# A new order of the SBUF tensors in a two-layer encoder trunk: activations on multiples of 2 KB, the places of the split weights staggered by 64 bytes

## The reference, cut to what matters

```python
for l in range(DEPTH):                       # DEPTH = 2
    u = x @ w_in[l]                          # 2048 -> 6144 (even) or 6152 (odd)
    # even: GLU + causal depthwise conv (31 taps) + LayerNorm + silu | HGRN2 heads
    # odd:  forgetting attention | chunked attention with relative bias
    mix = jnp.concatenate([a_out, b_out], axis=-1) @ w_out[l]    # 2048 -> 2048
    x = layer_norm(ALPHA * x + mix, ln_mix_g[l], ln_mix_b[l])
    h = jnp.square(jax.nn.relu(x @ mlp_w1[l])) @ mlp_w2[l]       # 2048 -> 8192 -> 2048
    x = layer_norm(ALPHA * x + h, ln_mlp_g[l], ln_mlp_b[l])
```

## Time and profile before

| | |
|---|---|
| median of 3 runs | 2315.05 us (2314.43 to 2316.96) |
| span of the profiled execution, first to last instruction | 2314.1 us |
| PE busy in the span | 2251.9 us (97%) |
| granted clock of TensorE, mean | 0.988 of full speed |
| memory read | 414.79 MB, 180 GB/s over the span |

### The profile page before, as it was taken

The page is one execution under the profiler, slowest core; times in us unless marked ns, Lnnn a source line. Parts: engine busy times, 40 slices in busy tenths (PEclk is TensorE's granted clock), DMA queues, the critical chain, the costliest instruction groups (busy, mean ns, idle before and its releaser), DMA issues.

```text
span 2314.1 us, 28894 instructions
## 1 busy us (share of the span) xinstructions
PE 2251.9 (97%) x10331; PEld 1868.4 (81%) x10331; DVE 1367.9 (59%) x1489; ACT 1068.1 (46%) x1163; POOL 34.1 (1%) x64
## 2 busy tenths in 40 slices
PE   8999999799999999999989999998999999999997
PEld 7888788688888888888878888887888888888885
DVE  4898986745545545545565545567455455455455
ACT  4555564354344344344344444434444444443543
POOL 2000000100000000000000000000000000000000
PEclk9999999899999999999999999999999999999998
DMA  7555545665665665666645555565656666656653
GB/s 240 170 158 158 170 127 177 190 197 189 192 189 185 191 190 183 197 184 189 193 156 162 166 180 164 168 192 177 188 189 194 184 190 193 184 189 194 188 188 122
DMA packets 213546, 418.70 MB, mean 181 GB/s; under 512 B 12777, under 2 KB 13857, under 8 KB 212400
## 3 DMA queue, kind: packets, MB, share of 16 engines
q1 hardware_dynamic: 211616, 406.90, 57.5%
q0 software_dynamic: 1808, 10.04, 1.2%
HBM read 414.79 MB, written 2.10 MB: 180 GB/s over the span
## 4 chain that ended last, share of the span: by engine, by line
PE 61%; issue 32%; DVE 5%; ACT 1%; DMA 1%; POOL 0%; POOLq 0%; SPq 0%; DVEq 0%; ACTq 0%
PE gemm L1210 19%; PE gemm L1212 19%; PE gemm L1211 19%; DVE lnp L969 1%; DVE w_lo L744 1%; PE pair L1330 1%; DMA raw<-in_ev_w_out 1%; DVE X L817 1%; DVE X L816 1%; PE pair L1563 1%; PE pair L1273 1%; ACT w_hi L440 0%; PE pair L1287 0%; PE pair L1403 0%; PE pair L1475 0%
## 5 line engine op out<-in xcount | busy, mean ns | idle before, releaser
L1084 DVE TENSOR_TENSOR w_lo<-raw,w_hi 128x1024 fp32r<-128x1024 f32 x508 | 621.6, 1224 | 663.2 <-ACT w_hi L647 663.2
L647 ACT ACTIVATE w_hi<-raw 128x1024 fp32r<-128x1024 f32 x508 | 537.8, 1060 | 774.5 <-PE gemm L1212 774.5
L1210 PE MATMUL gemm<-w_hi,x_hi 128*128 128x512 f32 x1792 | 710.5, 397 | 5.5 <-DVE w_lo L744 4.0
L1212 PE MATMUL gemm<-w_hi,x_lo 128*128 128x512 f32 x1792 | 702.2, 392 | 0.0
L1211 PE MATMUL gemm<-w_lo,x_hi 128*128 128x512 f32 x1792 | 701.7, 392 | 0.0
L1210 PE MATMUL gemm<-w_hi,c_hi 128*128 128x512 f32 x1280 | 500.8, 391 | 4.2 <-DVE X L772 2.5
L1212 PE MATMUL gemm<-w_hi,c_lo 128*128 128x512 f32 x1280 | 498.7, 390 | 0.0
L1211 PE MATMUL gemm<-w_lo,c_hi 128*128 128x512 f32 x1280 | 498.6, 389 | 0.0
L744 DVE TENSOR_TENSOR w_lo<-raw,w_hi 128x1024 fp32r<-128x1024 f32 x260 | 316.4, 1222 | 208.9 <-ACT w_hi L440 208.6
L440 ACT ACTIVATE w_hi<-raw 128x1024 fp32r<-128x1024 f32 x260 | 272.7, 1056 | 304.2 <-PE gemm L1212 276.8
L1210 PEld LDWEIGHTS gemm<-w_hi,x_hi 128*128 128x128 f32 x1792 | 339.2, 189 | 78.5 <-DVE w_lo L744 5.0
(11 more groups left out here) (195 smaller groups left out, 831.1 us busy)
## 6 DMA issues: line engine op xcount, KB each, us to landing
raw<-in_mlp_w SPq DMA_DIRECT2D x512, 512.0 KB, 3.9
raw<-in_ev_w_in SPq DMA_DIRECT2D x96, 512.0 KB, 3.7
raw<-in_od_w_in SPq DMA_DIRECT2D x96, 512.0 KB, 3.7
raw<-in_ev_w_out SPq DMA_DIRECT2D x32, 512.0 KB, 4.4
raw<-in_od_w_out SPq DMA_DIRECT2D x32, 512.0 KB, 4.4
lnp<-in_ln_mix_g POOLq DMA_DIRECT2D x2, 1024.0 KB, 5.9
lnp<-in_ln_mix_b POOLq DMA_DIRECT2D x2, 1024.0 KB, 9.2
lnp<-in_ln_mlp_g POOLq DMA_DIRECT2D x2, 1024.0 KB, 4.9
```

The source lines that it names most:

```text
L647: act.activation(w_hi[:, s % RING], raw[:, s % RING], ACT.Copy).then_inc(hi_ready, 1)
L1084: dve.tensor_tensor(w_lo[:, s % RING], raw[:, s % RING], w_hi[:, s % RING].bitcast(F32), ALU.subtract).then_inc(lo_ready, 1)
L1210: pe.matmul(acc[:, r, :], hi[:, k + c, rows], w_hi[:, slot, c, :], start=begin, stop=False)
L1212: ins = pe.matmul(acc[:, r, :], lo[:, k + c, rows], w_hi[:, slot, c, :], start=False, stop=end)
```

## The change

The tensors are allocated in a new order. The small ones come first, with `wf_hi` among them and an unused tensor `filler` of 64 bytes; their sizes on multiples of 32 bytes sum to 1920, so that behind the 128 bytes of constants `x_hi` starts on a multiple of 2 KB. `x_lo`, `c_hi`, `c_lo`, `raw`, `X` and `lnp` follow, all on multiples of 2 KB. Each of the four places of `w_hi` and of `w_lo` is now 4096 + 64 bytes long, so that place s starts 64 s bytes behind a multiple of 2 KB in `w_hi` and 256 + 64 s in `w_lo`; the 64 bytes between are not used. No instruction is added, removed or moved.

```diff
-        raw = sb("raw", [P, RING, CK, N], F32)
-        w_hi = sb("w_hi", [P, RING, CK, N], F32R)
-        w_lo = sb("w_lo", [P, RING, CK, N], F32R)
-        x_hi = sb("x_hi", [P, KT, S], F32R)
-        x_lo = sb("x_lo", [P, KT, S], F32R)
-        c_hi = sb("c_hi", [P, KT, S], F32R)
-        c_lo = sb("c_lo", [P, KT, S], F32R)
-        X = sb("X", [P, RT, D], F32)
-        lnp = sb("lnp", [P, 2, D], F32)
+
         ident = sb("ident", [P, P], F32)
         stats = sb("stats", [P, RT, NT, 6], F32)
         mv = sb("mv", [P, RT, 2], F32)
@@
         mhalf = sb("mhalf", [P, RT * HG], F32)
         factor = sb("factor", [P, FB], F32)
         nbias = sb("nbias", [P, RT], F32)
+        WF = KT * HEADS + P - HEADS
+        wf_hi = sb("wf_hi", [P, WF], F32R)
+        sb("filler", [P, 16], F32)
+        x_hi = sb("x_hi", [P, KT, S], F32R)
+        x_lo = sb("x_lo", [P, KT, S], F32R)
+        c_hi = sb("c_hi", [P, KT, S], F32R)
+        c_lo = sb("c_lo", [P, KT, S], F32R)
+        raw = sb("raw", [P, RING, CK, N], F32)
+        X = sb("X", [P, RT, D], F32)
+        lnp = sb("lnp", [P, 2, D], F32)
+
+        def places(name):
+
+            t = sb(name, [P, RING, CK * N + 16], F32R)
+            return t[:, :, 0:CK * N].rearrange("p q (c n) -> p q c n", c=CK)
+
+        w_hi, w_lo = places("w_hi"), places("w_lo")
         scr = sb("scr", [P, 14800], F32)
@@
-        WF = KT * HEADS + P - HEADS
         wf = cut(WF)
@@
-        wf_hi = sb("wf_hi", [P, WF], F32R)
         wf_lo = sb("wf_lo", [P, WF], F32R)
```

## The result

2346.65 us, median of 4 runs (2345.91 to 2351.71), against 2314.74 us of the kernel before, run beside it: ratio 1.0139, 95% interval 1.0124 to 1.0153. The change makes the kernel slower by 32 us. The forecast of 2286 us had the sign wrong, and the range, 2240 to 2340, missed the time by 7 us; the time lies between the two figures of the second rival (2338 and 2350).

A forecast was written before the change was run, and what follows sets the result against it. PE was taken to bound the kernel, through the spacing of 9216 weight matmuls at 226.6 ns. The terms summed as 2315.05 - 30.7 (placement) + 1.8 (given back in the even layer) = 2286 us, with a range of 2240 to 2340.

The forecast's parts named there:

- the second rival: Weight matmuls: changing offsets break the rhythm; 2338 us if each change costs 30 ns, 2350 if places 1-3 never settle; chance 0.25.
- What bounds the kernel: Whole kernel: PE bounds it, only the spacing of 9216 weight matmuls sets the products' time; an ns on each is 9.2 us.
- Whether the surplus hangs on addresses: Weight matmuls: the 13.3 ns each beyond pure columns, 123 us at most, was taken to depend on operand addresses modulo 256.
- The rival of no change: Weight matmuls: the 226.6 ns rhythm settles at any offset or the layout doesn't matter; 2315 us, within 5; chance 0.18.
- That PE's own two reads hinder each other: Weight matmuls: PE's read of the moving operand and its load of the next stationary one conflict, making the 13.3 ns surplus.
- Activations to multiples of 2 KB, place s at 64 s: Weight matmuls: places 0 to 3 save 0, 4.0, 4.3 and 5.0 ns, mean 3.3 ns, 30.7 us in all.
- offset 0: Matmul's moving start to next stationary start, modulo 256, is 0: slowest in the logits by 4 to 5 ns.
- it goes with the load, not with the columns: Matmuls of 256 and 512 columns: the surplus is the same for both, 13.2 and 13.3 ns, so the load sets it.
- the third rival: Weight matmuls: at three places of four the reads don't meet at all, 92 us less, 2223 us; chance 0.07.
- decisive figure of 227.1 ns: Weight matmuls: the mean spacing above which the second rival was to count as decided.
- What gives some back: Even layer: DVE's list doesn't shorten with the products, so PE may wait at the conv's end; 1.8 us, bounds 0 and 3.6.
- The splits, the taps, X and lnp: ACT and DVE work: splits cost nothing, taps at most 3.6 us either way, layer norms on X and lnp unchanged.

The follow-up runs named there:

- u192: Changed kernel without the stagger, all places of w_hi and w_lo 192 bytes behind a multiple of 2 KB: 2368.7 us, ratio 1.0233.
- u0: Changed kernel without the stagger, activations, raw, w_hi and w_lo all on multiples of 2 KB: 2314.1 us, ratio 0.9991.
- u256: Changed kernel without the stagger, all places of w_hi and w_lo 256 bytes behind a multiple of 2 KB: 2314.9 us.
- a64: Changed kernel without the stagger, activations 64 bytes behind a multiple of 2 KB, w_hi and w_lo on multiples of 256: 2367.8 us.
- u64: Changed kernel without the stagger, all places of w_hi and w_lo 64 bytes behind a multiple of 2 KB: 2330.4 us, ratio 1.0064.
- u128: Changed kernel without the stagger, all places of w_hi and w_lo 128 bytes behind a multiple of 2 KB: 2360.9 us, ratio 1.0199.
- h192: Distance 192 in all places, each weight matmul issued as two of 256 columns with its own load, from the changed kernel: 2363.7 us.
- bstag: Kernel before in its old order, with only the 64 bytes more in each place of w_hi and w_lo: 2350.8 us, ratio 1.0152.
- h0: Changed kernel without the stagger, distance 0, each weight matmul issued as two of 256 columns with its own load: 2435.1 us.
- p240: Changed kernel without the stagger, w_hi and w_lo placed inside larger tensors at distance 240 in all places: 2391.0 us.
- alt64: Changed kernel with places 0 and 2 at distance 0, places 1 and 3 at 64: 2341.8 us.
- lo64: Changed kernel without the stagger, w_hi at distance 0 and w_lo at 64 in every place: 2356.0 us.

## Why the prediction was wrong

**What bounds the kernel: right.** An ns per weight matmul is worth nearly 9.2 us: u192 against u0 has 6.4 ns x 9216 = 59 us of spacing and 54.6 us of time.

**Whether the surplus hangs on addresses: right, and the period too.** 256 (u256), the distance alone (a64), and the layout otherwise without effect (u0). The rival of no change is refuted by the same runs: with the same instructions the time goes from 2314 to 2391 us. That PE has two independent read ports and never waits on anyone, as the Trainium skill has it in "SBUF — State Buffer", "Who interferes with whom", is not what these runs show either.

**That PE's own two reads hinder each other: borne out.** In every run all the other large tensors, `raw` among them, moved together with the activations, so an interference of PE's reads with the accesses of DVE, ACT or the DMA engines would fit the times as well. The traces speak against it. In u192, from the first MLP on, the spacing is 233.3 ns where DVE and ACT are both busy throughout (533 spacings) and 233.5 where neither is (386); in u0 it is 227.2 (587) and 226.9 (168). With DMA transfers under way throughout, u192 has 233.3 ns (5011 spacings), and with almost none within half a us 233.3 (210). And in the logits only the stationary operands, in `wf_hi` and `wf_lo`, shift from step to step modulo 256.

**The failed step: "Activations to multiples of 2 KB, place s at 64 s", the term of -30.7 us.** It took the savings of 0, 4.0, 4.3 and 5.0 ns from the earlier trace rows, logit matmuls of 256 columns, and set them for matmuls of 512. The price at those four distances, measured at 512 columns, is 0, +2.1, +5.5 and +6.4 ns: u0, u64, u128, u192. In place of 3.3 ns saved on the mean, 3.5 ns are lost, and changing the distance costs 0.7 ns more. At 256 columns the reading of the rows held for the one distance tested, 192 (h192); 64 and 128 weren't run at that width. The prediction had seen that the surplus at offset 0 is the same 13 ns at both widths, and took this as leave to carry over the other offsets too; it holds for 0 and not for 192, the other distance run at both widths (120.0 ns is 13.3 over 106.7, 226.7 is 13.4 over 213.3; but at distance 192 the mean of 115.6 is 8.9 over, and 233.3 is 20.0 over). So "it goes with the load, not with the columns" fails there. (Where the prediction gives the bounds of this term, it says that the third rival prices a loss; it is the second that does.)

**The second rival, by its terms.** It had the sign and the size, but only the smaller part of the cause, so that its size came out partly by luck. The mean of the four uniform kernels is (226.9 + 229.0 + 232.4 + 233.3) / 4 = 230.4 ns: of the 4.25 ns over u0's 226.9, 3.5 are what the distances cost even if they never change. The rest, 0.75 ns or some 6 us over the 7680 matmuls behind the even layer, is what the changes cost, which it took for the whole. Its decisive figure of 227.1 ns was passed. The point held against it, that no logit at another offset is slower than at 0, was the same wrong transfer.

**What gives some back: right in kind, and for a loss as well.** 1536 of the 9216 weight matmuls run in the even layer, and there their spacings got longer by some 4 ns x 1536 = 6 us in all, but the MLP starts no later (455.4 against 457.2 us). That is why 4.1 ns make 32 us, not 38. How much the even layer takes up differs, though: from its first to its last weight matmul it takes 422.5 us before and 421.0 in the changed kernel, but 425.4 in bstag, with the same stagger; u192 has 425.8 against 420.3 in u0, 5.5 us for 9.9 us of spacing. That DVE's list sets the end there, busy for 217.8 of 252 us, fits, but no run shows it.

**The splits, the taps, X and lnp: right.** No group of ACT or DVE with 16 instructions or more moved by more than 5 ns on average, and the splits by about 1 ns.

**The range.** It took in the first form of the second rival (2338) and cut the second form off (2350); that form was the upper bound of the unknown cost, and the range should have reached it.

What stays open is how the two reads hinder each other, so that at 512 columns 0 is the best point and 16 bytes before it the worst, and that 32, 192 and 224 all sit at 233.3 ns. That the order of the distances turns round between 256 and 512 columns would fit an interference that depends on where in its operand the stream is while the load runs. This is only a guess: the loads' records last 189 ns beside a spacing of 227 (u0) and 193 beside one of 120 (h0), so they don't say which part of a matmul a load meets.

## What to carry to other kernels

Where TensorE sets the time and its matmul spacing is above the pure columns, the distance between the moving and the stationary operand's start, modulo 256 bytes, is a parameter worth a measurement: here it was worth up to 72 us (p240, 2391.0 against 2318.7 us of the kernel before beside it). Measure it at the width of the matmul itself, for the order of the distances turned round between 256 and 512 columns, and keep it the same from one matmul to the next. For 512 columns of float32r with a fresh 128-column stationary block each time, equal starts were the best of the eight distances run, and a stagger of the buffers was a loss.

## What was not expected of the hardware

- Two reads of one engine interfere by address: the mean spacing of the same matmuls goes from 226.9 to 235.8 ns with the distance modulo 256.
- Issued as two halves, each with its own load, the product costs 2 x 113.3 = 226.6 ns at distance 192 in the stretch shown of h192, as much as one matmul of 512 columns at distance 0, though it loads twice (2 x 117.8 = 235.6 at its other level). At distance 0 it costs 2 x 120.0 = 240 ns.
- Equal starts settle into one spacing (226, 227, 227 ns, nearly throughout the MLPs), and behind a disturbance find back to it within about six to ten matmuls; 64 has a cycle of three (226, 229, 232).
- A stream that changes its distance pays for the change: 2.5 ns per matmul between 0 and 64 with every chunk (alt64), 4.4 ns within every three matmuls (lo64), but only 0.75 ns in the changed kernel, half of whose distances are the slow ones.
